# Moving the weight splits and one head norm within the in-projection of a hybrid attention layer

## The chip, the core and the metric

The kernel runs on one core of a Trainium2 chip. It is one launch, and the metric is the device time of that launch in microseconds (us). The engines of the core are named as in the profile: PE (TensorE: matrix products, with its weight loads as PEld), DVE (VectorE), ACT (ScalarE), POOL (GpSimd) and SP (SyncE, which here only issues the loads of the weights). Each engine runs its own list of instructions in order; between engines there are only semaphores.

## What is computed

The reference runs a first stack of four layers over 272 tokens and then a second stack of two layers over 256 tokens, all with 1024 features in float32. The change is in the two layers of the second stack. Cut to what matters, one such layer is:

```python
def hybrid_mixer(h, w_in, rpb, q_norm, k_norm, w_out, rows, cos, sin):
    proj = h @ w_in
    na_q, na_k, na_v, g_q, g_k, g_v = jnp.split(proj, IN_SPLIT_POINTS, axis=-1)
    na_out = neighbourhood_attention(na_q, na_k, na_v, rpb, rows)        # 8 heads of 64, with a bias
    g_q = apply_axial_rope(rms_norm(g_q, q_norm), cos, sin)              # 8 query heads of 64
    g_k = apply_axial_rope(rms_norm(g_k, k_norm), cos, sin)              # 2 key heads
    gqa_out = gqa_block_attention(g_q, g_k, g_v)
    return jnp.concatenate([na_out, gqa_out], axis=-1) @ w_out

def memory_cross_attention(h, mem_n, w_q, w_kv, w_o):
    q = (h @ w_q)
    kv = (mem_n @ w_kv)
    ...
for l in range(DEPTH_2):
    x = x + hybrid_mixer(rms_norm(x, norm_mix[l]), w_in[l], ...)
    x = x + memory_cross_attention(rms_norm(x, norm_mem_q[l]), rms_norm(mem, norm_mem_kv[l]), ...)
    x = x + conv_ffn(rms_norm(x, norm_ffn[l]), ...)
```

## The kernel before

**Products in three passes.** Each float32 weight is split in two rounded parts: ACT copies `ring` to `ring_hi` (the high part), and DVE writes `ring - ring_hi` to `ring_lo` (the low part, line 2037). The moving side is split too, and PE makes three products for each piece of 128 by 128: high by high, high by low, low by high. A tile (128 output features for 256 tokens) takes 8 pieces, so 24 products. The weights come in blocks of four tiles (the block `in2b` has two) through a ring of four slots of half a block, each loaded by SP once PE has used what lay there. The split of block g+1 is made while PE works on block g. In the projections `in2_` and `memkv` it goes by quarters of a block, one for each tile (the function `hooks`, with `fine` true: 128x1024, or 128x512 where the next block is `in2b`); during the two tiles of `in2b` it goes by halves (128x2048).

**The stretch.** One layer's `in2_` (tiles 0 to 15), `in2b` (16, 17) and `memkv` (18 to 25) form one stretch of 26 tiles, and the attention of the layer is worked off in it, between tiles. `HYB_TILES` gives the order of the tiles (gk, gv, gq 0, gq 1, nv 0, nq 0, nk 0, gq 2, ...), and `hyb_steps` a list of steps for each half tile: half 2t is in the middle of tile t, half 2t+1 behind it. PE, ACT and DVE each walk the same lists and take out what is theirs. The steps that matter here are:
- `stat i`: PE sums the squares of head group i (0 is gk, 1 to 4 are gq), ACT turns the sum into a first root (`hrs`). In the half after it, `norm i` on DVE: three Newton operations (lines 2053, 2059, 2060) and the scaling of `raw` (2684). `partner i`: PE makes the rotated partner, DVE the rotation (2691 to 2693), whose end is `rope_ready`. PE may start the next step that uses bank 7 (a `stat`, a `partner`, or `tokens`, which turns values by line 1366) only when the step before it has left that bank; after a `partner`, this is `rope_ready`.
- `scores u` at half 15+2u: PE makes two products, DVE takes their minima (2705, or 2707 with a bias), ACT the exponentials with their sums. `scaled u` one half later: DVE's two reciprocals and scalings (2714, 2716). `turn u` three halves later: PE turns the probabilities (1386), ACT copies them (`ptok_ready`). `values u` four halves later: PE's products with the values. PE's `scores u+1` waits for the exponentials of `scores u`.

**Where the splits stand.** On ACT (line 1960) and on DVE (2738) tile t of the stretch begins with the split, `before(t - first)` or `after(t - first)`. The steps of halves 2t-1 and 2t follow, then (on DVE) the evacuation of tile t from PSUM, line 2754 or 2746, then (on ACT) the squares of a gk or gq tile. The accumulators alternate between two banks, so PE's tile t waits for the evacuation of tile t-2. DVE's low part of a piece waits for ACT's high part of the same piece.

Of the kernel before, what the change touches and what calls it, by code (L numbers as in the profile page):

```python
# [132 lines left out]
def hyb_steps(l):  # L133

    steps = {p: [] for p in range(HYB_END + 1)}
    for u, p in enumerate(HYB_SCORES):
        for later, name in [(0, "scores"), (1, "scaled"), (3, "turn"), (4, "values")]:
            steps[p + later].append((name, u))
        if u % 2:
            steps[p + 5].append(("gather", u // 2))  # L140
    order = ["gather", "values", "turn", "scores", "scaled"]
    for p in steps:
        steps[p].sort(key=lambda s: order.index(s[0]))
    for p, name, i in HYB_MISC:
        steps[p].append((name, i))
        if name == "stat":
            steps[p + 1].insert(0, ("norm", i))
    if l == 0:
        steps[MEMORY_SUM].append(("memory_sum", 0))
        steps[MEMORY_SUM + 1].insert(0, ("memory_root", 0))  # L150
    return steps
# [125 lines left out]
def build(nc, wt, xin, memin, params, consts, smallw, rpb, out):  # L277
    ctx = ExitStack()
    with ctx:
# [1206 lines left out]
        def _(act):  # L1486
# [427 lines left out]
            def hybrid(name, nb, tpb, before):  # L1914
# [39 lines left out]
                def at_half(p):  # L1954
                    for name, i in steps[p]:
                        if name in acts:
                            acts[name](i)

                for t in range(first, first + nb * tpb):
                    before(t - first)  # L1960
                    if t:
                        at_half(2 * t - 1)
                    at_half(2 * t)
                    part, c = (HYB_TILES + MEMORY_TILES)[t]
                    if part in ("gk", "gq"):
                        i = c + 1 if part == "gq" else 0
                        act.wait_ge(evacuated, BANKS + n.tile + t - first + 1)
                        if i >= 2:
                            act.wait_ge(hstat_ready, n.head + i - 1)
                        fn(sq[:, (n.head + i) % 2, 0:SEQ], raw[:, i % 3, 0:SEQ], ACT.Square).then_inc(hsq_ready, 1)  # L1970
# [47 lines left out]
        def _(v):  # L2018
# [657 lines left out]
            def hybrid(name, nb, tpb, after):  # L2676
# [58 lines left out]
                    new_rstd(SEQ)  # L2735
                    step(V.tensor_scalar(gain8[:, :], pcol(f"gqa_q{l}"), -0.125, None, ALU.mult))
                for t in range(first, first + nb * tpb):
                    after(t - first)
                    if t:
                        at_half(2 * t - 1)  # L2740
                    at_half(2 * t)
                    part, c = (HYB_TILES + MEMORY_TILES)[t]
                    v.wait_ge(acc_ready, n.tile + t - first + 1)
                    src = acc(n.tile + t - first, SEQ, P, 2)
                    if part == "nq":
                        V.scalar_tensor_tensor(out=a_nq[:, c, :], in0=src, scalar=-0.125, in1=rstd[:, 0:SEQ],
                                               op0=ALU.mult, op1=ALU.mult).then_inc(evacuated, 1)
                    else:
                        if part == "mk" and c == 0:
                            v.wait_ge(vt_ready, n.vtok + 5)  # L2750
                        dst = {"gk": raw[:, 0, 0:SEQ], "gq": raw[:, (c + 1) % 3, 0:SEQ], "gv": a_gv[:, :],
                               "nk": a_nk[:, c, :], "nv": a_nv[:, c, :], "mk": m_k[:, c, :], "mv": m_v[:, c, :]}[part]
                        by = mem_rstd if part in ("mk", "mv") else rstd
                        V.tensor_tensor(dst, src, by[:, 0:SEQ], ALU.mult).then_inc(evacuated, 1)
                n.tile += nb * tpb
                if name.startswith("memkv"):
                    at_half(HYB_END)
# [346 lines left out]
```

## Time and profile before

| | |
|---|---|
| three runs of the kernel before | 2367.93, 2375.32, 2377.53 us; median 2375.32 |
| the profiled execution | 2374.61 us, of which the profile's span is 2373.0 us |
| busy in it: PE / DVE / ACT / POOL | 2251.4 / 1555.9 / 1189.3 / 615.3 us |
| matmuls, mean granted clock | 19050, 0.985 |
| stretch of the first hybrid layer | from 1603.2 us (tile 1 begins at 1603.9) to 1729.0 us |
| stretch of the second hybrid layer | from 1985.7 to 2110.0 us |

The profile is one execution, so a time in it is good to what one execution is good to. PE is the engine that is almost always busy; what any other engine does costs time only where PE waits for it. A row of the timeline shows start and duration in us, then the instruction, and in brackets how long the engine sat idle before it and whose end released it. The granted clock (PEclk) is 1.00 at 2.4 GHz and 0.50 at 1.2 GHz. POOL's masking of the bias and its work on the memory (lines 2903 to 2945) run beside the first part of both stretches.

### The profile page before, as it was taken

The page shows a single profiled execution, that of the slowest core. Times are in us where ns is not written, and L with a number is a line of the kernel's source. Part 1 is how long each engine was busy: PE and PEld are TensorE (multiplying, and loading weights), DVE is VectorE, ACT ScalarE, POOL GpSimd, SP SyncE. Part 2 cuts the span into 40 slices and gives each one's busy share as a digit, 9 for nine tenths or more (in the row PEclk, how much of TensorE's full clock was granted, in tenths as well). Part 3 has the DMA queues.
Part 4 walks back from the last instruction along what each step waited for, and adds up shares of the span by engine and source line. Part 5 has one row for each costly group of instructions (what it writes and reads, how often), then busy time and mean ns, then how long its engine had stood idle before and what let it go on. Part 6 is the DMA issues. An engine that isn't in the chain of part 4 may idle for free.

```text
span 2373.0 us, 48140 instructions
## 1 busy us (share of the span) xinstructions
PE 2251.4 (95%) x19050; PEld 2141.5 (90%) x19050; DVE 1555.9 (66%) x2516; ACT 1189.3 (50%) x1848; POOL 615.3 (26%) x741
## 2 busy tenths in 40 slices
PE   5999999899999999899999999997999998899998
PEld 4889999899999788799998899997889998798998
DVE  5666554656555676565566665657768976767994
ACT  4555544445544652454445555444556544456553
POOL 4114211004111030031121142217135535033540
PEclk9999999999999998899999999999999999999999
DMA  4224545324546321145453245564354554343554
GB/s 190 89 90 160 177 155 184 123 89 161 177 153 196 114 73 55 54 164 175 161 175 107 89 159 181 171 202 147 110 187 158 180 170 167 103 135 127 188 168 134
DMA packets 52862, 344.02 MB, mean 145 GB/s; under 512 B 5904, under 2 KB 7120, under 8 KB 20176
## 3 DMA queue, kind: packets, MB, share of 16 engines
q1 hardware_dynamic: 51984, 336.26, 42.7%
q0 software_dynamic: 704, 5.31, 0.6%
q8 instruction: 125, 2.05, 0.3%
q14 instruction: 49, 0.40, 0.1%
HBM read 340.43 MB, written 1.05 MB: 144 GB/s over the span
## 4 chain that ended last, share of the span: by engine, by line
PE 73%; DVE 11%; ACT 7%; issue 5%; POOL 2%; DMA 1%; DVEq 0%; ACTq 0%; POOLq 0%
PE ps L767 72%; ACT ring_hi L1497 3%; DVE ring_lo L2037 3%; ACT arena L1497 2%; POOL arena L2938 1%; PE ps L959 1%; DVE newt L2059 1%; DVE arena L2151 1%; DVE newt L2053 1%; DVE hrs L2060 1%; ACT hrs L1497 0%; DMA ring<-in 0%; ACT sq L1497 0%; DMA ring<-out 0%; POOL arena_r L2939 0%
## 5 line engine op out<-in xcount | busy, mean ns | idle before, releaser
L767 PE MATMUL ps<-arena_r,ring_hi 128*128 128x272 f32 (+1 forms) x6688 | 1584.9, 286 | 7.5 <-DVE arena_r L2550 3.2
L767 PEld LDWEIGHTS ps<-arena_r,ring_hi 128*128 128x128 f32 x6688 | 1160.3, 190 | 15.6 <-issue 8.6
L767 PE MATMUL ps<-y_r,ring_hi 128*128 128x272 f32 (+1 forms) x3424 | 1008.8, 295 | 42.0 <-DVE ring_lo L2037 23.7
L2037 DVE TENSOR_TENSOR ring_lo<-ring,ring_hi 128x2048 fp32r<-128x2048 f32 (+2 forms) x372 | 740.5, 1992 | 378.8 <-ACT ring_hi L1497 378.0
L767 PE MATMUL ps<-y_r,ring_lo 128*128 128x272 f32 (+1 forms) x3424 | 978.3, 286 | 0.0
L767 PEld LDWEIGHTS ps<-y_r,ring_hi 128*128 128x128 f32 x3424 | 650.6, 190 | 66.2 <-issue 36.2
L1497 ACT ACTIVATE ring_hi<-ring 128x2048 fp32r<-128x2048 f32 (+2 forms) x372 | 611.4, 1647 | 111.1 <-DMA ring<-dn 52.0
L767 PEld LDWEIGHTS ps<-y_r,ring_lo 128*128 128x128 f32 x3424 | 652.7, 191 | 0.0
L767 PE MATMUL ps<-arena_r,ring_lo 128*128 128x256 f32 (+1 forms) x1632 | 463.9, 284 | 0.0
L767 PEld LDWEIGHTS ps<-arena_r,ring_lo 128*128 128x128 f32 x1632 | 307.9, 189 | 0.0
L1497 ACT ACTIVATE arena<-arena 128x272 f32<-128x272 f32 (+7 forms) x197 | 91.3, 466 | 395.6 <-DVE arena L2620 262.5
L2930 POOL CAST arena_r<-arena 128x272 fp32r<-128x272 f32 (+1 forms) x132 | 134.5, 1019 | 537.6 <-DVE arena L2622 417.1
L767 PE MATMUL ps<-arena 64*64 64x64 f32 (+18 forms) x2792 | 213.4, 263 | 16.0 <-ACT arena L1497 14.8
L767 PEld LDWEIGHTS ps<-arena 64*64 64x64 f32 (+10 forms) x2792 | 155.1, 143 | 55.7 <-issue 29.4
L2938 POOL TENSOR_SCALAR arena<-x,par 128x272 f32<-128x272 f32 (+1 forms) x98 | 94.1, 960 | 322.2 <-ACT y_r L1497 321.2
L1497 ACT ACTIVATE sq<-x 128x256 f32<-128x256 f32 (+1 forms) x120 | 50.2, 418 | 186.7 <-DVE x L2088 186.5
L1497 ACT ACTIVATE arena<-ps 128x256 f32<-128x256 f32 (+7 forms) x291 | 91.1, 363 | 71.1 <-PE ps L767 24.2
L2931 POOL TENSOR_TENSOR arena_r<-arena,arena_r 128x272 fp32r<-128x272 f32 (+1 forms) x132 | 102.3, 775 | 10.6
L2661 DVE SCALAR_TENSOR_TENSOR arena<-arena,par 128x256 f32<-128x256 f32 x176 | 99.4, 622 | 0.0
L1497 ACT ACTIVATE arena<-arena,par 128x256 f32<-128x256 f32 (+1 forms) x112 | 62.6, 583 | 66.4 <-DVE arena L2598 45.2
L2846 POOL TENSOR_SCALAR arena<-arena,row_inv 128x144 f32<-128x144 f32 (+2 forms) x72 | 33.2, 466 | 233.7 <-DVE row_inv L2198 233.5
L2088 DVE TENSOR_TENSOR x<-ps,x 128x256 f32<-128x256 f32 (+1 forms) x112 | 47.9, 428 | 63.9 <-PE ps L767 63.6
(233 smaller groups left out, 1688.1 us busy)
## 6 DMA issues: line engine op xcount, KB each, us to landing
ring<-gu SPq DMA_DIRECT2D x88, 1024.0 KB, 5.0
ring<-dn SPq DMA_DIRECT2D x64, 704.0 KB, 4.0
ring<-up SPq DMA_DIRECT2D x44, 1024.0 KB, 5.1
ring<-fox_in SPq DMA_DIRECT2D x32, 1024.0 KB, 5.0
ring<-sdn SPq DMA_DIRECT2D x32, 704.0 KB, 4.0
ring<-gdn_in SPq DMA_DIRECT2D x16, 1024.0 KB, 5.0
ring<-in SPq DMA_DIRECT2D x16, 1024.0 KB, 5.1
ring<-gla_in SPq DMA_DIRECT2D x12, 1024.0 KB, 5.1
```

The source lines that it names most:

```text
L767: return nc.tensor.matmul(dst, w, mv, start=start, stop=stop)
L959: last = nc.tensor.transpose(ps[0:w, 4 + u % 2, q * P:q * P + un["qn"]], un["p"][0:un["qn"], a:a + w], ident[0:un["qn"], 0:un["qn"]])
L1497: return nc.scalar.activation(dst, src, f, **kw)
L2037: V.tensor_tensor(ring_lo[:, slot, cols], ring[:, slot, cols], ring_hi[:, slot, cols].bitcast(F32), ALU.subtract).then_inc(lo_ready, 2 if ...
L2053: first = V.scalar_tensor_tensor(out=a, in0=square_sum, scalar=size * EPS, in1=r, op0=ALU.add, op1=ALU.mult)
L2059: step(V.scalar_tensor_tensor(out=b, in0=a, scalar=-0.5 / size, in1=r, op0=ALU.mult, op1=ALU.mult))
L2088: V.tensor_tensor(dst[:, c, :], take(c, width), dst[:, c, :], ALU.add).then_inc(evacuated, 1)
L2661: V.scalar_tensor_tensor(out=u_cc[:, q, :], in0=u_gp[:, q, 1 + tap:1 + tap + SEQ], scalar=par[:, bass.ds(i * 24 + (w0 + 12 * b + 3 * q + 1 ...
L2846: G.tensor_scalar(p, p, row_inv[0:un["qn"], u % 4:u % 4 + 1], 1.0, ALU.mult, ALU.mult).then_inc(p_ready, 1)
L2930: step(G.tensor_copy(hi_r[:, c, :], lo[:, c, :]))
L2931: G.tensor_tensor(lo_r[:, c, :], lo[:, c, :], hi_r[:, c, :].bitcast(F32), ALU.subtract).then_inc(h_split, 1)
L2938: step(G.tensor_scalar(lo[:, c, :], src[:, c, :], pcol(gain, c), 1.0, ALU.mult, ALU.mult))
```

## The change

Three edits in the functions that walk the stretch:
1. On DVE, the low part's split of tile t moves from the head of the tile's turn to its end, behind the evacuation.
2. On ACT, the high part's split of tile t moves from ahead of half 2t-1 to between the steps of half 2t-1 and those of half 2t.
3. In `hyb_steps`, `norm i` is put in behind as many places as the half has `scores` steps, instead of at its head. The norms stand in halves 4, 11, 15, 20 and 26. Scores stand in odd halves from 15 on, so of the five only `norm 2`, in half 15, changes its place; it now follows the minima of `scores 0`.

PE's, SP's and POOL's instructions keep their order, and no instruction is added or dropped.

```diff
--- before.py
+++ after.py
@@ -144,7 +144,7 @@
     for p, name, i in HYB_MISC:
         steps[p].append((name, i))
         if name == "stat":
-            steps[p + 1].insert(0, ("norm", i))
+            steps[p + 1].insert(sum(step == "scores" for step, _ in steps[p + 1]), ("norm", i))
     if l == 0:
         steps[MEMORY_SUM].append(("memory_sum", 0))
         steps[MEMORY_SUM + 1].insert(0, ("memory_root", 0))
@@ -1957,9 +1957,9 @@
                             acts[name](i)
 
                 for t in range(first, first + nb * tpb):
-                    before(t - first)
                     if t:
                         at_half(2 * t - 1)
+                    before(t - first)
                     at_half(2 * t)
                     part, c = (HYB_TILES + MEMORY_TILES)[t]
                     if part in ("gk", "gq"):
@@ -2735,7 +2735,6 @@
                     new_rstd(SEQ)
                     step(V.tensor_scalar(gain8[:, :], pcol(f"gqa_q{l}"), -0.125, None, ALU.mult))
                 for t in range(first, first + nb * tpb):
-                    after(t - first)
                     if t:
                         at_half(2 * t - 1)
                     at_half(2 * t)
@@ -2752,6 +2751,7 @@
                                "nk": a_nk[:, c, :], "nv": a_nv[:, c, :], "mk": m_k[:, c, :], "mv": m_v[:, c, :]}[part]
                         by = mem_rstd if part in ("mk", "mv") else rstd
                         V.tensor_tensor(dst, src, by[:, 0:SEQ], ALU.mult).then_inc(evacuated, 1)
+                    after(t - first)
                 n.tile += nb * tpb
                 if name.startswith("memkv"):
                     at_half(HYB_END)
```

DVE at the start of the first hybrid layer, before (L2754 is the evacuation of tiles 0 and 1, L2037 the low part):

```order
L2736 TENSOR_SCALAR gain<-par 128x1
L2037 TENSOR_TENSOR ring_lo<-ring,ring_hi 128x1024
L2754 TENSOR_TENSOR raw<-ps,rstd 128x256
L2037 TENSOR_TENSOR ring_lo<-ring,ring_hi 128x1024
L2754 TENSOR_TENSOR arena<-ps,rstd 128x256
L2037 TENSOR_TENSOR ring_lo<-ring,ring_hi 128x1024
L2053 SCALAR_TENSOR_TENSOR newt<-ps,hrs 128x256
```
and now (the evacuation is L2753 there):

```order
L2736 TENSOR_SCALAR gain<-par 128x1
L2753 TENSOR_TENSOR raw<-ps,rstd 128x256
L2037 TENSOR_TENSOR ring_lo<-ring,ring_hi 128x1024
L2753 TENSOR_TENSOR arena<-ps,rstd 128x256
L2037 TENSOR_TENSOR ring_lo<-ring,ring_hi 128x1024
L2053 SCALAR_TENSOR_TENSOR newt<-ps,hrs 128x256
```
Each evacuation stands one split earlier; the split of tile t now stands where that of tile t+1 stood.

DVE at tile 8, where `scores 0` (L2705) stands, before:

```order
L2754 TENSOR_TENSOR raw<-ps,rstd 128x256
L2037 TENSOR_TENSOR ring_lo<-ring,ring_hi 128x1024
L2053 SCALAR_TENSOR_TENSOR newt<-ps,hrs 128x256
L2059 SCALAR_TENSOR_TENSOR newt<-newt,hrs 128x256
L2060 SCALAR_TENSOR_TENSOR hrs<-newt,hrs 128x256
L2684 SCALAR_TENSOR_TENSOR raw<-raw,gain,hrs 128x256
L2705 TENSOR_REDUCE neg_max<-ps 128x1 x2
L2714 RECIPROCAL row_inv<-row_sum 128x1
L2716 TENSOR_SCALAR arena<-arena,row_inv 128x256
L2714 RECIPROCAL row_inv<-row_sum 128x1
L2716 TENSOR_SCALAR arena<-arena,row_inv 128x256
L2754 TENSOR_TENSOR arena<-ps,rstd 128x256
```
and now:

```order
L2753 TENSOR_TENSOR raw<-ps,rstd 128x256
L2037 TENSOR_TENSOR ring_lo<-ring,ring_hi 128x1024
L2705 TENSOR_REDUCE neg_max<-ps 128x1 x2
L2053 SCALAR_TENSOR_TENSOR newt<-ps,hrs 128x256
L2059 SCALAR_TENSOR_TENSOR newt<-newt,hrs 128x256
L2060 SCALAR_TENSOR_TENSOR hrs<-newt,hrs 128x256
L2684 SCALAR_TENSOR_TENSOR raw<-raw,gain,hrs 128x256
L2714 RECIPROCAL row_inv<-row_sum 128x1
L2716 TENSOR_SCALAR arena<-arena,row_inv 128x256
L2714 RECIPROCAL row_inv<-row_sum 128x1
L2716 TENSOR_SCALAR arena<-arena,row_inv 128x256
L2753 TENSOR_TENSOR arena<-ps,rstd 128x256
```
The minima come ahead of the four operations of `norm 2`; the two scalings (L2716) still follow both, and the split ahead of them is that of tile 7 instead of tile 8.

ACT at tiles 8 and 9, before (`sq` is the square of gq 2, `row_sum` marks the exponentials, 128x512 is the copy of turned probabilities):

```order
L1497 ACTIVATE ring_hi<-ring 128x1024
L1497 ACTIVATE arena,row_sum<-ps,neg_max 128x256 x2
L1497 ACTIVATE ring_hi<-ring 128x1024
L1497 ACTIVATE arena,row_sum<-ps,neg_max 128x256 x2
L1497 ACTIVATE arena<-ps 128x512
L1497 ACTIVATE arena<-ps 128x2x128
L1497 ACTIVATE ring_hi<-ring 128x1024
```
and now:

```order
L1497 ACTIVATE sq<-raw 128x256
L1497 ACTIVATE arena,row_sum<-ps,neg_max 128x256 x2
L1497 ACTIVATE ring_hi<-ring 128x1024
L1497 ACTIVATE arena,row_sum<-ps,neg_max 128x256 x2
L1497 ACTIVATE ring_hi<-ring 128x1024
L1497 ACTIVATE arena<-ps 128x512
L1497 ACTIVATE arena<-ps 128x2x128
```
The exponentials come ahead of the high part, and the copy of the turned probabilities comes behind one.

## Rows read from the trace of the kernel before

**Rows 1.** The page, first part: busy time (share of the span), instructions.
```profile
PE 2251.4 (95%) x19050; PEld 2141.5 (90%) x19050; DVE 1555.9 (66%) x2516; ACT 1189.3 (50%) x1848; POOL 615.3 (26%) x741
```

**Rows 2.** Waits of PE, 1592 to 1706 us: total, times, longest.
```profile
PE ps L767 <- ACT arena L1497: 7.7, 6, 4.0
PE ps L767 <- DVE arena L2693: 3.2, 2, 2.2
PE ps L767 <- ACT sq L1497: 1.9, 1, 1.9
```

**Rows 3.** Waits of PE, 1980 to 2110 us, same columns.
```profile
PE ps L767 <- ACT arena L1497: 5.9, 4, 2.8
PE ps L767 <- ACT sq L1497: 2.8, 1, 2.8
PE ps L767 <- DVE arena L2693: 2.1, 2, 1.3
```

**Rows 4.** Timeline, DVE: start, duration (us), instruction, [idle before]; first tiles.
```profile
1606.91 1.22 DVE L2037 TENSOR_TENSOR ring_lo<-ring,ring_hi 128x1024 fp32r<-128x1024 f32 x1
1608.06 0.42 DVE L2754 TENSOR_TENSOR raw<-ps,rstd 128x256 f32<-128x256 f32 x1
1609.90 1.23 DVE L2037 TENSOR_TENSOR ring_lo<-ring,ring_hi 128x1024 fp32r<-128x1024 f32 x1 [1.43 <-ACT ring_hi L1497]
...
1990.58 1.44 DVE L2037 TENSOR_TENSOR ring_lo<-ring,ring_hi 128x1024 fp32r<-128x1024 f32 x1
```

**Rows 5.** Timeline, PE: the steps that waited, and the token turns of nv0.
```profile
1608.97 0.70 PE L767 MATMUL ps<-sq,con 128*128 128x256 f32 x2 [1.87 <-ACT sq L1497]
...
1622.44 0.70 PE L767 MATMUL ps<-sq,con 128*128 128x256 f32 x2 [2.24 <-DVE arena L2693]
...
1641.88 1.11 PE L767 MATMUL ps<-arena 64*128 64x256 f32 x4 [4.02 <-ACT arena L1497]
...
1646.50 0.38 PE L1366 MATMUL ps<-con,arena 128*128 128x128 f32 x2
...
1992.85 0.48 PE L767 MATMUL ps<-sq,con 128*128 128x256 f32 x1 [2.77 <-ACT sq L1497]
...
2006.90 0.70 PE L767 MATMUL ps<-sq,con 128*128 128x256 f32 x2 [1.27 <-DVE arena L2693]
...
2024.59 0.80 PE L767 MATMUL ps<-arena 64*128 64x256 f32 x2 [2.84 <-ACT arena L1497]
...
2029.07 0.38 PE L1366 MATMUL ps<-con,arena 128*128 128x128 f32 x2
```

**Rows 6.** Timeline, DVE, around the first minima (L2705) and the third rotation (L2693).
```profile
1636.18 1.58 DVE L2037 TENSOR_TENSOR ring_lo<-ring,ring_hi 128x1024 fp32r<-128x1024 f32 x1 [1.44 <-ACT ring_hi L1497]
...
1640.28 0.74 DVE L2705 TENSOR_REDUCE neg_max<-ps 128x1 f32<-128x256 f32 x2
1641.32 0.17 DVE L2714 RECIPROCAL row_inv<-row_sum 128x1 f32<-128x1 f32 x1 [0.30 <-ACT arena L1497]
...
1645.34 0.63 DVE L2693 TENSOR_TENSOR arena<-arena,sqsum 128x256 f32<-128x256 f32 x1
...
2028.02 0.42 DVE L2693 TENSOR_TENSOR arena<-arena,sqsum 128x256 f32<-128x256 f32 x1
```

**Rows 7.** Stretches: us, busy (x) by engine, PEclk, DMA share, GB/s.
```profile
1642.00:1646.00 4.00, 4.00 (x18) 3.17 (x19) 3.91 (x8) 1.71 (x5) 3.70 (x6) 0.57 0.01 4
1994.00:1997.00 3.00, 3.00 (x16) 3.00 (x15) 3.00 (x4) 1.47 (x3) 3.00 (x2) 0.50 0.11 46
1997.00:2000.00 3.00, 3.00 (x28) 3.00 (x27) 2.16 (x5) 0.70 (x2) 2.70 (x6) 0.99 0.02 5
```

**Rows 8.** Timeline, ACT: a copy of turned probabilities, the high part behind it.
```profile
1710.78 0.60 ACT L1497 ACTIVATE arena<-ps 128x512 f32<-128x512 f32 x1 [0.30 <-issue]
1711.27 1.05 ACT L1497 ACTIVATE ring_hi<-ring 128x1024 fp32r<-128x1024 f32 x1
```

**Rows 9.** Timeline, PE: the values step that takes this copy.
```profile
1712.03 0.66 PE L767 MATMUL ps<-arena 128*64 128x128 f32 x8
```

## Prediction

> **What bounds the kernel now.** I read the page first. PE is busy for 2251.4 of 2373.0 us [rows 1], so only time in which PE waits, or runs at half clock, can be won. The change touches two stretches, one for each hybrid layer, and I asked next what PE waits for in each. In the first, the three largest items are 7.7 us for ACT, 3.2 for the rotation on DVE (L2693) and 1.9 for ACT's squares [rows 2]; in the second they are 5.9, 2.8 and 2.1 [rows 3]. That is 23.6 us together, 1.0% of the run, and it is nearly all that can be gained. Then I looked at where these waits lie. The long ones are all in the first half of a stretch, where the attention starts up: 1.87, 2.24 and 4.02 us in the first layer, 2.77, 1.27 and 2.84 us in the second [rows 5]. Behind each lies the same picture on DVE: its split of the low part stands ahead of what PE wants, and before that split DVE sits idle for 1.43 or 1.44 us until ACT has made the high part of the same piece [rows 4, 6]. DVE does so four times in each layer before the first attention minima.
>
> The clock matters too. After the wait of 4.02 us PE runs at a granted 0.57 in the four microseconds that follow, and after the one of 2.77 us at 0.50 for three; in those three it starts 16 products, in the next three, at 0.99, it starts 28 [rows 7]. So half clock costs about 3 x 12/28 = 1.3 us in a stretch of 3, and about 1.5 for a whole fall. Such a fall follows the three longest waits of the two stretches (the wait of 2.84 us too) and none that is 2.24 us or shorter.
>
> **Part 1: the low part behind the evacuation.** DVE's order is a chain of evacuation, split, evacuation, split either way. What changes is which piece is split in which place: always the one before. So no DVE time is saved, but two things are. The first evacuation loses the split ahead of it, and ACT has had a whole tile's time to make the high part, so the idle 1.43 us go.
>
> First layer. The first evacuation starts at 1606.91 instead of 1608.06, so the squares and PE's `stat 0` come 1.15 us earlier [rows 4]. The wait of 1.87 us at 1608.97 [rows 5] shrinks to 0.7. Before `stat 1` PE waits 2.24 us for the first rotation. Three idle spells of 1.4 us on DVE lay on the way to that; without them the rotation would come 1.15 + 4.3 = 5.4 us earlier, but it can't start before PE's `partner 0`, which is only 1.15 earlier. By the durations in the trace it ends about 1.0 us ahead of PE's need, so all 2.24 go. PE is now 3.4 us ahead. The next two waits (for `norm 1` and for the second rotation) have DVE working without a pause ahead of them, and I give 0.1 for them: 3.5 us ahead.
>
> Second layer. The same two terms are 1.44 - 0.07 = 1.37 (a split's duration less the overlap with the next instruction, which is 1.22 - 1.15 in the first layer) and 1.27 [rows 4, 5]. The first wait falls from 2.77 to 1.4 us, shorter than several after which the clock did not fall. So I take the fall as gone, which gives 1.5 us more. With 0.25 at `norm 1` PE is 4.4 us ahead.
>
> **Part 2: the minima ahead of `norm 2`.** In the first layer DVE's split of tile 8 waits 1.44 us and takes 1.58, from 1636.18; then four operations of the norm fill the time to the minima at 1640.28, 2.6 us [rows 6]. PE waits 4.02 us for the exponentials of these minima, at 1641.88, that is 1.60 us behind their start [rows 5, 6]. Now the 1.44 and the 2.6 both go from ahead of the minima. That is 4.04 against 4.02, so this wait vanishes, in the second layer too, and with it the fall of the clock.
>
> But the norm is not gone, it stands behind the minima, and PE needs it in its very next step (`partner 2`), and then the third rotation before it may turn the tokens of nv0. From the split at tile 8 to that rotation's end DVE holds the same work in either order. It loses only its pauses: the 1.44, the 0.30 ahead of the reciprocal [rows 6] and some 0.1 more. In the old order PE came to its token turn at 1646.50, while the rotation ended at 1645.34 + 0.63 = 1645.97, so 0.53 us of slack are used up as well [rows 5, 6]. PE reaches its token turn ahead by 3.5 + 1.44 + 0.4 + 0.53 = 5.9 us, and not by 3.5 + 4.0 and the clock's fall. The rest comes back as two new waits: about 1.0 us ahead of `partner 2` and 2.6 us ahead of the token turn. In the second layer the slack is 2029.07 - (2028.02 + 0.42) = 0.63 [rows 5, 6], and PE is ahead by 4.4 + 1.43 + 0.4 + 0.63 = 6.9 us, with new waits of 0.2 and 2.2 us.
>
> **Part 3: the high part between the halves, on ACT.** Here the change takes something. From tile 9 on the exponentials come first, then the high part, then the copy of the turned probabilities that PE's next `values` step takes. In the steady part the copy starts at 1710.78, after 0.30 us of idle time, lasts 0.60, and PE takes it at 1712.03 [rows 8, 9]. A high part of 1.05 us [rows 8], of which 0.1 overlaps the next instruction, fills the 0.30 and delays the copy by 0.65. The copy then ends at 1712.03, just when PE wants it: cost nothing, but no slack is left. Where ACT is later than that, at three or four steps of a layer, I find 0.2 to 0.5 us lost. Against it, at tiles 11 and 15 to 18 DVE loses five pauses of 0.4 to 1.5 us, so minima come 0.5 to 1.8 us earlier. The two halves of 1.9 us on ACT (tiles 16, 17) stand ahead of a copy now, but ahead of them the minima come 1.8 earlier, and the two cancel. The sum is +0.2 us a layer, and bounds from these numbers are -2.5 and +1.5.
>
> Low parts stay in time: a piece is used three tiles after the tile it is split in, and for `in2b` and the first half of `memkv`, where it is one or two tiles, the split ends 3 us or more ahead. The loads are issued by PE's progress and move with it, and nothing behind the stretch is tied to a fixed time.
>
> **POOL.** Its work beside the stretch does not move, and PE reaches each tile 6 us earlier, so more of DVE's work falls beside it. The last operation of the rotation takes 0.63 us in the first layer, with POOL at work, and 0.42 in the second, where POOL has finished [rows 6]. A few such operations on the path cost about 0.5 us in all. The Trainium skill (SBUF, State Buffer, section "Who interferes with whom") says that a DVE instruction with two SBUF inputs contends with a GpSimd instruction that reads SBUF, and that the loser blocks for a whole instruction. The two rows agree with it. If each of some ten two-input operations that newly lie beside POOL lost 0.2 us on the path, the cost would be 2 us instead of 0.5.
>
> **The sum**, against the profiled execution: 5.9 + 6.9 + 2 x 0.2 - 0.5 = 12.7 us, of 2374.61: **2362 us**. The median of the three runs is 2375.32, 0.7 higher, so this is 0.56% below the median.
>
> **Rivals.**
> *A. The new waits bring the clock down.* PE now waits 1.0 and, 1.6 us later, 2.6 us in the first layer, and 2.2 in the second. Falls came after 2.77 us and more, none after 2.24, so the first layer's pair is near the edge. One fall costs 1.5 us, two 3: 2363.5 to 2365. The Trainium skill (TensorE: Matmul & The Clock Gate, section "HAM oscillation") warns of just this, idle gaps that put the array back to half rate again and again; in this trace the falls follow the longest gaps, as it says.
> *B. ACT becomes the one that is late.* If the copies come 0.3 us later than I reckon in ten steps of each layer, 6 us are lost: about 2368. For it speaks that no slack is left in the steady part; against it, that the minima come earlier wherever DVE had paused.
> *C. Slower.* The price of C is the whole high part at each of the 15 copies of a layer: 30 x 1.05 = 31.5 us, less the 12.7: 2393 us. It decides where a copy has less than 0.65 us between its end and PE's `values` step. The steady rows show just 0.65 (1712.03 - 1710.78 - 0.60), so each step would have to lose nearly all of its 1.05, which rows 8 and 9 speak against.
> *D. The pauses stay.* The change would do nothing if ACT made the high part as late as before. But ACT is idle ahead of most of its high parts in this order, and the list shows each one placed a tile ahead of its low part. 2374 us.
> *E. More is won.* If the DVE work between minima and rotation runs as fast in the first layer as in the second, and the ACT part costs nothing, PE gains 2 to 3 us more: 2359.5.
>
> **Chances.** The forecast 0.42, A 0.24, B 0.14, E 0.12, D 0.04, C 0.04. A measurement of this kernel tells about 0.5% from no change, and 0.5% below 2375.32 is 2363.4, 1.4 us from my forecast. So I split: of the forecast and A together 0.66, some 0.39 lies below that line and 0.27 above; E is below it; B and D are within; C is above. This gives faster 0.51, same 0.45, slower 0.04. The range, from E with a little below it to B: 2358 to 2368.5.
>
> **What would show it.** In the profile after: no pause of 1.4 us on DVE for `ring_hi` in the first eight tiles; the wait ahead of `stat 0` about 0.7 and 1.4 us, none ahead of `stat 1`, none ahead of `scores 1`; new waits of PE for L2684 (ahead of `partner 2`) and for L2693 (at the token turn, L1366), 1 and 2.6 us in the first layer; the first stretch about 6 us shorter, the second 7; a granted clock of 1.00 ahead of tile 2 of the second layer. It would be wrong if PE waited for ACT at most `values` steps, or if the waits for the rotation were longer than 3 us.

## The result, and the profile after

| | before | after |
|---|---|---|
| median, same runs | 2368.09 us (7 runs, 2365.01 to 2377.53) | 2357.85 us (7 runs, 2352.71 to 2365.01) |
| profiled execution, span | 2373.0 us | 2356.2 us |
| mean granted clock | 0.985 | 0.989 |

The ratio is 0.9947, 95% interval 0.9925 to 0.9969: 0.53% faster, where the prediction said 0.56%. In absolute terms the 2357.85 us lie 4.2 us below the forecast of 2362.0 and 0.15 us below the lower end of the range. The ratio is taken over all 14 runs and isn't the quotient of the two medians, which are 10.2 us, 0.43%, apart. The two statements differ because the forecast subtracted its 12.7 us from the one profiled execution of the kernel before, 2374.61 us, and the seven runs here, of which that forecast knew three, have a median of 2368.09.

The first part of the page after, which answers [rows 1], and its line for the low part's split (busy, mean ns, idle time before it):

```profile
PE 2241.9 (95%) x19050; PEld 2133.4 (91%) x19050; DVE 1554.9 (66%) x2516; ACT 1188.1 (50%) x1848; POOL 616.9 (26%) x741
...
L2037 DVE TENSOR_TENSOR ring_lo<-ring,ring_hi 128x2048 fp32r<-128x2048 f32 (+2 forms) x372 | 739.8, 1990 | 359.7 <-ACT ring_hi L1497 359.2
```

The work of DVE, ACT and POOL is what it was. PE is busy 9.5 us less for the same instructions, at a higher mean clock. The idle time before the splits is 359.7 us, 378.8 on the page before. What PE waits for, 1590 to 1700 us (answers [rows 2]) and 1965 to 2100 us (answers [rows 3]); total, times, longest:

```profile
PE ps L767 <- ACT arena L1497: 5.2, 8, 1.2
PE ps L1366 <- DVE arena L2693: 2.6, 1, 2.6
PE ps L767 <- DVE raw L2684: 1.8, 2, 1.6
PE ps L767 <- DVE arena L2693: 1.2, 1, 1.2
PE ps L767 <- ACT sq L1497: 0.7, 1, 0.7
```
```profile
PE ps L767 <- ACT arena L1497: 3.0, 5, 1.2
PE ps L1366 <- DVE arena L2693: 1.6, 1, 1.6
PE ps L767 <- DVE raw L2684: 1.4, 1, 1.4
PE ps L767 <- ACT sq L1497: 1.4, 1, 1.4
PE ps L767 <- DVE arena L2693: 0.8, 1, 0.8
```

The items read like those of before, but the ACT item is another thing now. The wait of 4.0 us for the first exponentials was in it; that one is gone, and eight waits of up to 1.2 us for copies stand there. The same on PE's timeline, which answers [rows 5] (`stat 0`, `stat 1`, `partner 1`, `stat 2`, `scores 1`, `partner 2`, the turn of nv0; then `stat 0` and the turn in the second layer):

```profile
1597.82 0.70 PE L767 MATMUL ps<-sq,con 128*128 128x256 f32 x2 [0.73 <-ACT sq L1497]
...
1608.88 0.59 PE L767 MATMUL ps<-sq,con 128*128 128x256 f32 x2
...
1615.28 0.67 PE L767 MATMUL ps<-raw,con 128*128 128x256 f32 x2 [1.58 <-DVE raw L2684]
1618.53 0.70 PE L767 MATMUL ps<-sq,con 128*128 128x256 f32 x2 [1.16 <-DVE arena L2693]
...
1624.22 0.70 PE L767 MATMUL ps<-arena 64*128 64x256 f32 x4
...
1625.19 0.67 PE L767 MATMUL ps<-raw,con 128*128 128x256 f32 x2 [0.26 <-DVE raw L2684]
...
1630.26 0.44 PE L1366 MATMUL ps<-con,arena 128*128 128x128 f32 x2 [2.56 <-DVE arena L2693]
...
1980.31 0.70 PE L767 MATMUL ps<-sq,con 128*128 128x256 f32 x2 [1.42 <-ACT sq L1497]
...
2011.00 0.44 PE L1366 MATMUL ps<-con,arena 128*128 128x128 f32 x2 [1.56 <-DVE arena L2693]
```

DVE's timeline, first tiles and around the first minima (answers [rows 4, 6]):

```profile
1596.89 0.42 DVE L2753 TENSOR_TENSOR raw<-ps,rstd 128x256 f32<-128x256 f32 x1
1597.23 1.21 DVE L2037 TENSOR_TENSOR ring_lo<-ring,ring_hi 128x1024 fp32r<-128x1024 f32 x1
1598.37 0.42 DVE L2753 TENSOR_TENSOR arena<-ps,rstd 128x256 f32<-128x256 f32 x1
1598.75 1.22 DVE L2037 TENSOR_TENSOR ring_lo<-ring,ring_hi 128x1024 fp32r<-128x1024 f32 x1
...
1621.09 1.22 DVE L2037 TENSOR_TENSOR ring_lo<-ring,ring_hi 128x1024 fp32r<-128x1024 f32 x1
1622.22 0.75 DVE L2705 TENSOR_REDUCE neg_max<-ps 128x1 f32<-128x256 f32 x2
...
1629.71 0.50 DVE L2693 TENSOR_TENSOR arena<-arena,sqsum 128x256 f32<-128x256 f32 x1
```

No split waits for its high part, and the minima follow theirs without the four operations of the norm between. The rotation ends at 1630.21, and PE's turn starts at 1630.26: this chain on DVE is what PE now waits for.

The clock ahead of tile 2 of the second layer, where [rows 7] had 16 products in 3 us at 0.50 (columns as there):

```profile
1982.00:1985.00 3.00, 3.00 (x28) 3.00 (x27) 2.90 (x5) 0.97 (x2) 3.00 (x4) 1.00 0.35 147
```

**A measure that is free of the rest of the run.** Two executions of this program differ by some us in places where nothing was changed. So I measured each stretch by itself, from the end of its tile 1 to the first product of the out-projection, and summed PE's waits in it over 0.15 us (without the one of 0.52 us that every kernel has just ahead of that last product). The falls of the clock inside it are counted from the granted clock.

| kernel | first stretch begins | first stretch, us | waits | falls | second, us | waits | falls |
|---|---|---|---|---|---|---|---|
| before | 1607.10 | 122.46 | 15.17 | 1 | 120.43 | 12.29 | 2 |
| after | 1597.09 | 117.11 | 11.53 | 0 | 113.47 | 8.27 | 0 |
| h1_all_again (= after) | 1594.98 | 119.87 | 12.78 | 1 | 113.52 | 8.28 | 0 |
| g1_low | 1594.82 | 115.82 | 10.08 | 0 | 111.56 | 6.38 | 0 |
| g2_norm | 1595.42 | 123.41 | 14.45 | 2 | 119.37 | 12.43 | 1 |
| g3_low_norm | 1603.87 | 114.68 | 8.98 | 0 | 110.51 | 5.47 | 0 |
| h2_low_norm_tokens | 1597.85 | 116.59 | 9.19 | 1 | 112.30 | 5.86 | 1 |
| h3_high_late | 1599.77 | 118.95 | 11.79 | 1 | 113.10 | 7.84 | 0 |
| i1_halves_early | 1599.47 | 115.99 | 10.47 | 0 | 112.55 | 7.43 | 0 |
| i2_low_first_tiles | 1603.36 | 119.23 | 12.02 | 1 | 115.98 | 9.50 | 1 |
| i3_low_high | 1597.25 | 117.93 | 10.72 | 1 | 114.59 | 9.34 | 0 |

Take the waits from the length. Without a fall 105.5 to 105.7 us are left in the first stretch (4 kernels) and 105.0 to 105.3 in the second (7 kernels), with one fall 107.1 to 107.4 and 106.4 to 106.9, with two 109.0 and 108.1. So a stretch is a fixed part, the same to 0.3 us in every kernel, plus its waits plus 1.2 to 1.8 us for each fall. The change took 5.35 and 6.96 us: in the first stretch 3.64 of waits and 1.7 for one fall, in the second 4.02 of waits and 2.9 for two falls. Together that is 12.3 us. The two profiles also differ by 10.0 us ahead of the first stretch and by 5.5 the other way between and behind the stretches, where after has 264.7 us from the first stretch to the second, with 10.2 us of it at half clock, and before 260.5 without any; h1_all_again, the same program as after, has 260.3 there. These parts move from execution to execution, and nothing here shows a share of the change in them.

### The profile page after: what moved, and what is told of

It reads as the page before. It is cut to its first block, busy times and chain, and to the rows that moved or that the text cites. A ratio compares the mean times of both kernels' runs of the same rounds, so it can differ in the third digit from the quotient of the medians.

```text
span 2356.2 us, 48140 instructions
## 1 busy us (share of the span) xinstructions
PE 2241.9 (95%) x19050; PEld 2133.4 (91%) x19050; DVE 1554.9 (66%) x2516; ACT 1188.1 (50%) x1848; POOL 616.9 (26%) x741
## 3 DMA queue, kind: packets, MB, share of 16 engines
HBM read 340.43 MB, written 1.05 MB: 145 GB/s over the span
## 4 chain that ended last, share of the span: by engine, by line
PE 76%; DVE 10%; ACT 6%; issue 4%; POOL 2%; DMA 1%; DVEq 0%; ACTq 0%; POOLq 0%
PE ps L767 74%; ACT ring_hi L1497 3%; DVE ring_lo L2037 2%; ACT arena L1497 2%; POOL arena L2938 1%; PE ps L959 1%; DVE newt L2059 1%; DVE arena L2151 1%; DVE newt L2053 0%; DVE hrs L2060 0%; ACT hrs L1497 0%; DMA ring<-in 0%; DMA ring<-out 0%; POOL arena_r L2939 0%; PE ps L1386 0%
## 5 line engine op out<-in xcount | busy, mean ns | idle before, releaser
L2037 DVE TENSOR_TENSOR ring_lo<-ring,ring_hi 128x2048 fp32r<-128x2048 f32 (+2 forms) x372 | 739.8, 1990 | 359.7 <-ACT ring_hi L1497 359.2
L1497 ACT ACTIVATE arena<-arena,neg_max 128x144 f32<-128x144 f32 (+3 forms) x104 | 47.7, 459 | 83.3 <-DVE neg_max L2188 50.3
```

The lines of the kernel that those rows point to most:

```text
L1497: return nc.scalar.activation(dst, src, f, **kw)
L2037: V.tensor_tensor(ring_lo[:, slot, cols], ring[:, slot, cols], ring_hi[:, slot, cols].bitcast(F32), ALU.subtract).then_inc(lo_ready, 2 if ...
```

## Experiments

Each was timed beside the kernel before. The sizes I use are the stretches of its one profile, from the table; the time of the whole run (medians of 4 to 10 runs) moves with falls elsewhere. The same program repeats its waits to 0.01 us in the second stretch and to 1.25 us in the first (after and h1_all_again), so a difference of a microsecond is read from the second. The median of the kernel before beside them was 2370.24 (g), 2369.50 (h) and 2369.61 us (i), of 13 runs each.

**The first edit alone.** DVE's split behind the evacuation, in the form that both g1 and g3 have:

```diff
                 for t in range(first, first + nb * tpb):
-                    after(t - first)
                     if t:
                         at_half(2 * t - 1)
...
                         V.tensor_tensor(dst, src, by[:, 0:SEQ], ALU.mult).then_inc(evacuated, 1)
+                    after(t - first)
```


> Only the first edit: the low part on DVE behind the evacuation; ACT's order and the norm's place are as before. I compare two stretches of PE, from the end of tile 1 (start of the first head statistic less its wait) to the first product of the out-projection: 122.5 us in the first hybrid layer before and 117.1 with the whole change, 120.4 and 113.5 in the second. Theory (DVE's pauses for ACT are what was won): the pauses of 1.4 us go, the wait ahead of the first exponentials shrinks only from 4.0 to about 2.5 us, but the third rotation comes as early as without its 0.4 us: stretches 5.5 and 6.4 us shorter than before, and up to 1 us more each, since no high part stands ahead of a copy on ACT. Rival (the minima ahead of the norm win most): 3.5 and 4.4 us. Time about 12 us below before by the theory, 8 by the rival.

2348.17 us, ratio 0.991 [0.989, 0.993]; stretches 6.6 and 8.9 us shorter than before. By the stretches this edit alone gives more than all three. The whole run fell by 22.1 us between the medians, 6.6 more than the 15.5 of the stretches; where that came from was not traced. In the first layer, the waits at `stat 0`, `stat 1` and the first exponentials shrink to 0.74, none and 1.85 us, and in both layers together the three falls go. PE's waits for copies in the second stretch (0.65, 0.96, 1.49 us) go as well, which the prediction had not counted.

**The third edit alone.**

```diff
-            steps[p + 1].insert(0, ("norm", i))
+            steps[p + 1].insert(sum(step == "scores" for step, _ in steps[p + 1]), ("norm", i))
```


> Only the third edit: norm 2 behind the minima of scores 0. Theory: the long wait shrinks by 2.6 us and its clock fall goes, but PE then waits for the third rotation, whose DVE work is the same, so each stretch is only about 1 us shorter (0.3 of pause and 0.5 to 0.6 of slack). Rival: what the long wait loses is kept, 4 us in each stretch. Time 2 us below before by the theory, 8 by the rival.

2366.87 us, ratio 0.9987 [0.9973, 1.0001]; stretches +0.95 and -1.06 us. The wait of 4.02 us becomes three, of 1.07, 1.08 and 0.77 us (`scores 1`, `partner 2`, the turn). The waits of the first stretch are 0.7 us fewer, but two falls lie in it where before had one; in the second the waits are 0.1 us more and a fall fewer. The ratio can't be told from 1, and the 1 us a stretch of the theory isn't shown. One of the falls (granted clock 0.50 from 1631 to 1634) came behind the first two of the three new waits, 1.07 and 1.08 us. Moving the norm behind the minima passes DVE's work on to the next two steps of PE.

**The first and the third, ACT left as it was.**

> First and third edit, ACT's order as before. With the whole change PE waits 5.2 us in the first and 3.0 us in the second stretch for ACT, mostly for copies of turned probabilities that now stand behind a high part. Theory: these copies come about 0.5 to 1 us earlier at some five steps, so the stretches are 1 to 2.5 us shorter than with the whole change (115 to 116 and 111.5 to 112.5 us), time about 15 us below before. Rival (the high part ahead of the exponentials would only move the wait to the exponentials): no shorter than with the whole change, 117.1 and 113.5.

2352.29 us, ratio 0.9923 [0.9907, 0.994]; stretches 114.68 and 110.51. That is 1.14 and 1.05 us below g1: this is what the norm's place is worth. And it is 2.43 and 2.96 us below the whole change, so the second edit, the high part between the halves, costs that much (the figures of the second layer are the firm ones). The rows show how. In the changed kernel the copy of the turned probabilities stands behind a high part, and PE waits 1.24 us for it:

```profile
1642.23 1.05 ACT L1497 ACTIVATE ring_hi<-ring 128x1024 fp32r<-128x1024 f32 x1
1643.18 0.59 ACT L1497 ACTIVATE arena<-ps 128x512 f32<-128x512 f32 x1
```
```profile
1643.82 1.29 PE L767 MATMUL ps<-arena 128*64 128x128 f32 x12 [1.24 <-ACT arena L1497]
```
In g3_low_norm the copy of the same step follows the exponentials:

```profile
1649.43 0.20 ACT L1497 ACTIVATION_READ_ACCUMULATOR arena<-ps,neg_max 128x1 f32 x1
1649.52 0.59 ACT L1497 ACTIVATE arena<-ps 128x512 f32<-128x512 f32 x1
```
```profile
1650.17 1.29 PE L767 MATMUL ps<-arena 128*64 128x128 f32 x12 [0.79 <-ACT arena L1497]
```
PE still waits 0.79 us at this step. All of PE's waits for ACT's copies: 3.02 us in the second stretch of after (five), none in that of g3_low_norm.

The second edit alone was not tried, and by the order of the lists it can't run: ACT's high part would wait behind exponentials, whose minima stand on DVE behind the low part of the same piece, so each would wait for the other. It needs the first edit.

**The whole change once more**, to tell the base from the stretches.

> The changed kernel, once more. Theory (the two stretches give the whole gain, and the rest of the difference between two executions comes from falls of the clock that lie elsewhere): the first stretch, from the end of its tile 1 to the first product of the out-projection, takes 117.1 us again and the second 113.5, each within 0.7, while the time at which the first one begins (1597.09 us before) may differ by several us. Rival (the change also shortens what lies ahead of the stretches, 10.0 us between the two first profiles): the first stretch begins at 1597.1 within 1 again, and the kernel is 20 us faster in every profile.

2354.97 us, ratio 0.9939 [0.9918, 0.9961]. The second stretch is the same to 0.05 us. The first is 2.76 us longer, more than the 0.7 I allowed: 1.25 us of waits and a fall of the clock behind the wait at the turn. Columns: stretch in us, length, busy (x instructions) of PE, PEld, DVE, ACT, POOL, granted clock, DMA share, GB/s. First h1_all_again, whose turn started at 1629.53 after 2.71 us, then after, whose turn started at 1630.26 after 2.56 us:

```profile
1630.00:1633.00 3.00, 3.00 (x20) 2.70 (x18) 1.37 (x5) 0.55 (x2) 2.70 (x7) 0.53 0.00 0
```
```profile
1630.50:1633.50 3.00, 3.00 (x27) 2.37 (x26) 2.58 (x5) 0.94 (x3) 2.77 (x5) 1.00 0.22 20
```
So rival A of the prediction is real: the same kernel shows it in one execution and not in the other. The run's median is 14.5 us below that of the kernel before, the first measurement's was 10.2; the 12.3 of the stretches lies between. Its beginning at 1594.98 against 1597.09 says no more than that the start moves; over all eleven profiles, whose programs are the same up to there, it lies between 1594.82 and 1607.10.

**The turn of nv0 later** (on top of g3_low_norm).

```diff
-HYB_MISC = [(3, "stat", 0), (6, "tokens", 0), (8, "partner", 0), (10, "stat", 1), (13, "partner", 1), (14, "stat", 2), (17, "partner", 2), (18, "tokens", 1),
-            (19, "stat", 3), (22, "partner", 3), (23, "tokens", 2), (25, "stat", 4), (28, "partner", 4), (29, "tokens", 3), (33, "tokens", 4)]
+HYB_MISC = [(3, "stat", 0), (6, "tokens", 0), (8, "partner", 0), (10, "stat", 1), (13, "partner", 1), (14, "stat", 2), (17, "partner", 2),
+            (19, "stat", 3), (21, "tokens", 1), (22, "partner", 3), (23, "tokens", 2), (25, "stat", 4), (28, "partner", 4), (29, "tokens", 3), (33, "tokens", 4)]
```


> The low part behind the evacuation and the norm behind the minima, ACT as in the kernel before, and the turn of nv0's tokens moved from half 18 to half 21, behind the sum of squares of the next group. Theory (the wait of 2.55 us in the first layer and of 1.57 in the second at this turn is a wait for the third rotation that anything else can cover): the sum of squares in half 19 comes about 1 us of PE work later than the token turn does now, so 1 us of the wait is covered and no more unless other products lie between; the stretches take 113.6 and 109.5 us (114.68 and 110.51 with the turn in half 18). Rival 1 (half a tile of products, 2.5 us, comes to lie ahead of the wait): 112.1 and 109.0. Rival 2 (the wait is only passed on, since the next rotation is late too): 114.7 and 110.5.

2350.71 us, ratio 0.9916 [0.9895, 0.9937]; stretches 116.59 and 112.30, each with a fall. The theory doesn't hold. The wait is only passed on, as in rival 2, but not for its reason: the waits at the turn (2.55, 1.57) go, and `partner 3` waits 2.46 and 1.95 us, not for a rotation but for ACT's copy of these tokens, which in its new half stands behind exponentials. The second layer, PE, then ACT, then the stretch behind it:

```profile
2017.63 0.70 PE L767 MATMUL ps<-raw,con 128*128 128x256 f32 x2 [1.95 <-ACT arena L1497]
```
```profile
2016.28 0.47 ACT L1497 ACTIVATE arena<-ps,neg_max 128x256 f32<-128x256 f32 x1 [3.23 <-DVE neg_max L2705]
...
2017.19 0.86 ACT L1497 ACTIVATE arena<-ps 128x256 f32<-128x256 f32 x2
```
```profile
2019.00:2022.00 3.00, 3.00 (x19) 2.21 (x17) 2.11 (x4) 0.94 (x2) 0.00 (x0) 0.50 0.22 35
```

**The high part behind both halves**, so behind the copy (on top of the whole change).

```diff
                     if t:
                         at_half(2 * t - 1)
-                    before(t - first)
                     at_half(2 * t)
+                    before(t - first)
```


> All of the change, but ACT's high part of tile t stands behind the steps of both halves, 2t-1 and 2t, and so behind the copy of the turned probabilities. Theory (the 2.4 and 3.0 us that the high part's new place costs are lost because it stands ahead of that copy): stretches of 114.7 and 110.5 us, within 0.6, as with ACT left as it was, and no wait of PE for ACT over 0.9 us at the values steps. Rival 1 (they are lost because the high part is later at all, so the low part and the DVE work behind it are later): 117.1 and 113.5 or more. Rival 2 (the square of a gk or gq tile now stands behind the high part, 1.05 us later): 1 us more for each of the five sums of squares that PE waits for, 116 and 112.

2358.60 us, ratio 0.9957 [0.9939, 0.9975]; stretches 118.95 (one fall) and 113.10. Rival 1 holds: the copy has its old place back, and the second stretch gains only 0.4 of 3.0 us. Now DVE's split waits for the high part, and the minima behind it are late, so that PE waits 1.32 us at the `values` step behind them:

```profile
2056.56 2.29 DVE L2037 TENSOR_TENSOR ring_lo<-ring,ring_hi 128x2048 fp32r<-128x2048 f32 x1 [1.35 <-ACT ring_hi L1497]
2058.77 0.75 DVE L2705 TENSOR_REDUCE neg_max<-ps 128x1 f32<-128x256 f32 x2
```
On ACT's list each high part here stands ahead of exponentials again, but it is that of the tile before. So of the three places tried one is good: ahead of the exponentials, where ACT waits for DVE anyway, and a tile's steps ahead of its low part. Between the halves it delays the copy, behind them it delays the low part.

**The two long high parts early**, the others as in the change.

```diff
                 for t in range(first, first + nb * tpb):
+                    if t in (16, 17):
+                        before(t - first)
                     if t:
                         at_half(2 * t - 1)
-                    before(t - first)
+                    if t not in (16, 17):
+                        before(t - first)
```


> All of the change, but for the two half blocks (the high parts of 1.9 us, at tiles 16 and 17) ACT keeps the order of the kernel before: high part at the head of the tile. Theory (each high part delays the copy behind it by what it has no slack for, so the two long ones cost most: 0.60 and 1.21 us of the 3.0 us of the second stretch): the two waits go, the others (0.17, 0.48, 0.57) stay, and the second stretch takes 113.5 - 1.8 = 111.7 us, the first 117.1 - 1.8 = 115.3 plus about 1.6 if a clock fall lies in it. Rival (the loss comes from somewhere else, and the long ones only show it): 113.5 and 117.1, with the same sum of waits of PE for ACT at the values steps, 3.0 us in the second stretch.

2355.15 us, ratio 0.9934 [0.9909, 0.9958]; stretches 115.99 and 112.55, 1.1 and 0.9 us shorter than after, half of what I expected. The waits of 0.60 and 1.21 us go, but the next copy, behind the first short high part, has one of 0.93 us. PE is earlier there, and the copy isn't. The theory is right in kind, and its size is only an upper bound: a part of a wait that is taken away reappears at the next place without slack.

**The low part behind the evacuation in tiles 0 to 8 only** (on top of g3_low_norm).

```diff
                 for t in range(first, first + nb * tpb):
+                    if t > 8:
+                        after(t - first)
                     if t:
                         at_half(2 * t - 1)
...
-                    after(t - first)
+                    if t <= 8:
+                        after(t - first)
```


> The low part behind the evacuation only in tiles 0 to 8, at the head of the tile from tile 9 on; the norm behind the minima, ACT as in the kernel before. Theory (the later tiles matter too: behind the evacuation the split no longer holds up the minima, so that the exponentials and the copies are earlier): the waits of PE for ACT at the values steps come back as they were in the kernel before, 3.1 us in the second stretch (0.65, 0.96, 1.49) against none, and 3.7 in the first against 1.8, so the stretches take 116.6 and 113.6 us. Rival (the whole gain lies in the first eight tiles): 114.7 and 110.5, as with the split behind the evacuation throughout.

2363.60 us, ratio 0.9971 [0.9955, 0.9986]; stretches 119.23 and 115.98, each with a fall. The waits for copies come back, 0.67, 0.96 and 1.49 us in the second stretch (0.65, 0.96 and 1.49 before):

```profile
PE ps L767 <- ACT arena L1497: 3.1, 3, 1.5
PE ps L1366 <- DVE arena L2693: 2.7, 1, 2.7
```
That is the theory. The second line is an effect of the seam that I had missed: at tile 9 two splits stand in a row ahead of the rotation, and the wait at the turn grows from 1.57 to 2.70 us (first layer 2.55 to 3.88).

**The first and second edit.**

> The low part behind the evacuation and the high part between the halves, the norm at the head of its half as in the kernel before. Theory (the place of the norm is worth the same 1.1 us with either order on ACT): stretches of 118.2 and 114.5 us where the whole change takes 117.1 and 113.5, with a wait of PE for the first exponentials of about 2 us and a shorter one at the token turn. Rival 1 (with the high part behind the exponentials the norm's place is worth more, since DVE's split in front of it waits for ACT): 120 and 117. Rival 2 (nothing): 117.1 and 113.5.

2355.08 us, ratio 0.9935 [0.9909, 0.9961]; stretches 117.93 (one fall) and 114.59. The second is 1.1 us over the whole change, as the theory says. In the first the waits are 0.8 us fewer than with the whole change, although the wait for the exponentials is back (1.85 us). The fall fits this, in one pair of profiles: it comes behind this wait, PE is slow on its way to the turn and doesn't wait there, where g1_low, without a fall, waits 1.78 us.

```profile
1626.38 0.70 PE L767 MATMUL ps<-arena 64*128 64x256 f32 x4 [1.85 <-ACT arena L1497]
...
1631.21 0.44 PE L1366 MATMUL ps<-con,arena 128*128 128x128 f32 x2
```
```profile
1628.00:1631.00 3.00, 3.00 (x15) 2.78 (x14) 2.96 (x6) 1.34 (x5) 2.77 (x4) 0.51 0.02 5
```
Here the wait paid for a part of the fall ahead of it.

## Why the prediction had the gain right and the time wrong

**The base was the step that failed.** Of the sum "12.7 us, of 2374.61" the first term was nearly right: the two stretches became 5.35 + 6.96 = 12.3 us shorter. The second was mis-sized: the kernel before measured 2368.09 us as the median of seven runs, 6.5 us less, and 2369.6 as that of 13 later ones. The sum had been set against the one profiled execution and its neighbourhood of three runs. By the granted clock, PE in that execution stood at 1.2 GHz for 54.6 us ahead of the first stretch, where the ten other profiles, whose instructions up to there are the same, have 23.9 to 41.0. Over the eleven profiles the beginning of the stretch moves by 0.43 us for each us at half clock (a straight line through them), and before is the latest of all, 1607.10. Of the 16.8 us between the two first profiles, 10.0 arose ahead of the changed code. From 2368.09 the same 12.7 us would have given 2355.4, from 2369.6 it would have given 2356.9; measured were 2357.85 and, in h1, 2354.97. The range took in the doubt in the change's terms and left out the doubt in the base. The three runs shown already spread over 9.6 us, nearly as much as the whole range.

**The gain by parts.** Up to the turn of nv0 the sum was close. Counted from the beginning of the stretch, PE reached that turn 6.2 us earlier in the first layer (5.9 forecast) and 6.9 in the second (6.9). From there on the first stretch lost 0.9 us and the second won 0.1, where part 3 had +0.2 us for each. That the total came within 0.4 us of 12.7 is in part luck: the two large effects of the steady half, in Part 3 below, were each missed and nearly cancel.

**Part 1: right, and too small.** The waits at `stat 0` came out as forecast, 0.73 (0.7) and 1.42 (1.4), that at `stat 1` vanished in both layers, and in the second layer the fall behind `stat 0` went too. At `norm 1` the second layer did not win the 0.25 us of the forecast: that wait grew from 1.24 to 1.43. What the part left out is the steady half of the stretch. Behind the evacuation the split no longer stands ahead of the minima, and i2 against g3 shows its worth: 3.1 us of waits for copies in the second layer.

**Part 2: right in its mechanism.** The wait for the exponentials vanished with its fall, the work came back as a wait at the turn: 2.56 us (2.6 forecast) and 1.56 (2.2); ahead of `partner 2` 0.26 (1.0) and none (0.2). The forecast of these waits didn't fit its own terms: 3.5 + 4.0 + 1.5 for the fall less the 5.9 leaves 3.1 us for the two waits of the first layer, not 3.6, and 2.82 were measured; the second layer's terms leave 4.4 + 2.84 + 1.5 - 6.9 = 1.8, not 2.4, and 1.56 were measured. That "the norm is not gone" was the important sentence: the norm's place is worth 1.1 us a layer beside the first edit, and the first edit alone had already taken 2.2 of the 4.02 us.

**Part 3: wrong by 1.7 us in the first layer, and near in the second by errors that cancel.** PE's waits for copies went from 3.69 to 5.22 us in the first stretch and from 3.10 to 3.02 in the second. That is a loss of 1.5 us and a gain of 0.1, where the sum had a gain of 0.2 each. (A later wait for a rotation, 0.70 us in the first stretch and 0.24 in the second, went too; the forecast hadn't counted it.) But g3 against after shows that these are -1.9 and -3.1 us through the low part and +3.4 and +3.0 through the high part. A step that failed is "the two cancel" at tiles 16 and 17: behind the long high parts PE waits 0.60 and 1.21 us. Another is "at three or four steps of a layer, 0.2 to 0.5 us": there were six such waits in the first stretch and three in the second, of 0.17 to 1.24 us. The steady row on which it rested [rows 8, 9] had just no slack left, and I took it for free.

**POOL.** The 0.5 us can't be told apart. In h1 the waits for `norm 1` and `norm 2` of the first layer were 2.00 and 1.29 us, against 1.58 and 0.26 in after with the same instructions. For `norm 2` the 1.03 us lie in the length of three of DVE's four operations. Two of them, first in after, then in h1_all_again:

```profile
1623.33 0.42 DVE L2059 SCALAR_TENSOR_TENSOR newt<-newt,hrs 128x256 f32<-128x256 f32 x1
1624.54 0.50 DVE L2684 SCALAR_TENSOR_TENSOR raw<-raw,gain,hrs 128x256 f32<-128x256 f32 x1
```
```profile
1621.41 1.00 DVE L2059 SCALAR_TENSOR_TENSOR newt<-newt,hrs 128x256 f32<-128x256 f32 x1
1623.32 0.83 DVE L2684 SCALAR_TENSOR_TENSOR raw<-raw,gain,hrs 128x256 f32<-128x256 f32 x1
```
The third is L2060, 0.72 and 0.84 us; the fourth, L2053, which reads one of its operands from PSUM, took 0.41 in both. POOL was at work all this time, and its masking had begun 7.1 us behind the beginning of the stretch in after and 6.1 in h1 (a load releases it), so the two engines met at other instants. In the second layer an operation of DVE releases POOL. There it works until 2005.4 us in after, beside `norm 1` too, and the waits still repeat to 0.01 us. That POOL lengthens DVE's operations in the first layer fits all this; without a run that takes POOL's work away it is argued, not shown.

**Clock, rival A.** "Falls came after 2.77 us and more, none after 2.24" does not hold. There was none after 2.55 and 2.56 us (g3, after), and one after 2.71 (h1), 1.95 (h2) and 1.85 (i3), and in g2 one behind two waits of 1.07 and 1.08. The length of one wait doesn't decide it. The section "HAM oscillation" of the Trainium skill (TensorE: Matmul & The Clock Gate) warns that idle gaps can bring the array to half rate; these runs agree that falls follow gaps and show that one can't be promised or excluded from a gap's length. The price of 1.5 us was right (1.2 to 1.8).

**The other rivals.** B was right about the place, the copies on ACT, and near in its price (6 us in all; 5.4 measured, most of it hidden by the unforecast gain). C did not come: the new place of the high parts costs 5.4 us in both layers together, not 31.5. D fell: no pause for the high part is left in the first eight tiles. E gave the nearest time, 2359.5, but not by its mechanism.

**A better version** is the first edit alone, 0.991 of before [0.989, 0.993], or with the norm moved too, 0.9923 [0.9907, 0.994]. By the stretches, with no fall in any of the four, the second is the shorter, by 1.1 us a layer; the runs can't separate them.

## What to carry to other kernels

When work moves between in-order queues, ask for each piece where its engine waits anyway, and whether the piece is still in time for its reader. Here that is behind the evacuation on DVE, and ahead of the exponentials on ACT, so one half of a symmetric-looking change won 15 us in the two stretches (4.6 of them by falls that went) and the other gave 5 back. Sum a changed stretch by itself as work plus waits plus clock falls, and forecast a ratio or give the base its own range: the unchanged part ahead of the stretches varied by 12.3 us, as much as the change was worth.

## What the hardware showed that was not expected

- Identical instructions from the start of the run to the first changed one took 1594.8 to 1607.1 us, with 23.9 to 54.6 us of it at a granted clock of 0.50.
- One fall of the clock costs PE 1.2 to 1.8 us net in these stretches, and it may come behind a wait of 1.85 us, or two of 1.07 and 1.08, in one kernel and stay away behind 2.56 us in another, or come in one execution of a program and not in the next.
- A fall can shorten the next wait: in i3_low_high the wait at the turn (1.78 us in g1_low) was gone behind a fall.
- The same DVE operation over two operands in SBUF took 0.42 us in one execution and 1.00 us in the next, with POOL at work beside it in both.
